# Hybrid diffusion step with mixture of experts: expert 2 loaded before the router has decided, the last two experts returned by one product, and products of constants in TensorE's waits

## The reference, cut to what matters

```python
h = _rms(x, p['norm2']) * (1 + sc2) + sh2
x = x + g2 * _hier_moe(h, p)
# _hier_moe: 4 groups x 4 experts; a token takes the best group, and in it the top 2 experts
gl = (h @ p['w_group_router']).astype(jnp.float32)
g_sel = jax.nn.one_hot(jnp.argmax(gl, axis=-1), N_GROUPS, dtype=jnp.float32)
top_v, top_i = lax.top_k(el_sel, TOP_K)
...
for gi in range(N_GROUPS):
    a = jnp.einsum('bsd,edf->bsef', h, p['w_e1'][gi])        # 1024 x 512 for each expert
    b = jnp.einsum('bsd,edf->bsef', h, p['w_e3'][gi])        # 1024 x 512
    y = y + jnp.einsum('bsef,efd->bsd', jax.nn.silu(a) * b * w_all[:, :, gi, :, None], p['w_e2'][gi])
```

## Time and profile before

| | us |
|---|---|
| median of 3 runs (1882.34 to 1887.23) | 1882.98 |
| the profiled execution, its own time | 1894.46 |
| its span in the profile | 1892.7 |
| PE busy in the span | 1782.1 (94%) |
| DVE, ACT, POOL busy | 813.7, 442.7, 122.4 |
| expert stage of layer 0, first hidden(0) product to last returned chunk | 704.5 to 976.0 |
| the same, layer 1 | 1607.8 to 1880.7 |

### The profile page before, as it was taken

The page is one execution under the profiler, slowest core; times in us unless marked ns, Lnnn a source line. Parts: engine busy times, 40 slices in busy tenths (PEclk is TensorE's granted clock), DMA queues, the critical chain, the costliest instruction groups (busy, mean ns, idle before and its releaser), DMA issues.

```text
span 1892.7 us, 25310 instructions
## 1 busy us (share of the span) xinstructions
PE 1782.1 (94%) x10202; PEld 1095.7 (58%) x10202; DVE 813.7 (43%) x1850; ACT 442.7 (23%) x956; POOL 122.4 (6%) x160
## 2 busy tenths in 40 slices
PE   6999999999999989997789999999999998999887
PEld 3445656688777773332245565667888877333223
DVE  1295473565544451111133966536655455111113
ACT  3312344333100121010043134334321112111002
POOL 0001201000000030000020020010000003000002
PEclk9999999999999989998989999999999998999988
DMA  9662293413556658999952221323123335899994
GB/s 403 224 261 91 95 361 106 156 68 112 198 221 270 245 200 353 425 427 426 424 209 101 110 94 58 131 93 120 69 90 112 133 151 201 326 424 425 428 427 156
DMA packets 51926, 422.42 MB, mean 223 GB/s; under 512 B 6448, under 2 KB 7872, under 8 KB 28768
## 3 DMA queue, kind: packets, MB, share of 16 engines
q1 hardware_dynamic: 33696, 369.35, 48.9%
q0 software_dynamic: 9632, 33.07, 5.1%
q10 hardware_dynamic: 8480, 18.35, 2.6%
HBM read 386.38 MB, written 32.28 MB: 221 GB/s over the span
## 4 chain that ended last, share of the span: by engine, by line
PE 81%; DMA 14%; another core or an unknown queue 1%; issue 1%; DVE 1%; ACT 1%; SPq 0%; POOL 0%; ACTq 0%; DVEq 0%
PE psum L871 19%; PE psum L1148 19%; PE psum L1137 9%; PE psum L1319 8%; PE psum L874 7%; DMA pc<-we_in 6%; DMA ring<-we_in 6%; PE psum L1340 2%; PE psum L791 2%; PE psum L1324 2%; DMA ring<-wch_in 2%; PE psum L849 1%; PE psum L1223 1%; PE psum L1335 1%
## 5 line engine op out<-in xcount | busy, mean ns | idle before, releaser
L871 PE MATMUL psum<-hT,ring 128*128 128x384 f32 x1088 | 363.9, 489 | 0.1
L871 PEld LDWEIGHTS psum<-hT,ring 128*128 128x128 f32 x1088 | 202.9, 190 | 141.2 <-issue 12.4
L1137 PE MATMUL psum<-pc,ring 128*128 128x384 f32 x512 | 175.6, 486 | 0.0
L1319 PE MATMUL psum<-ring,scr 128*64 128x512 f32 x512 | 126.9, 653 | 30.9 <-DMA ring<-we_in 27.1
L2625 DVE TENSOR_TENSOR ytok<-pc,psum 128x256 f32<-128x256 f32 (+1 forms) x32 | 15.1, 471 | 323.1 <-ACT pc L1815 323.1
L1148 PE MATMUL psum<-hT,ring 128*128 128x192 f32 x768 | 143.0, 329 | 1.8 <-ACT vals L1514 1.8
L1148 PEld LDWEIGHTS psum<-hT,ring 128*128 128x128 f32 x768 | 126.1, 190 | 18.6 <-issue 9.6
L1319 PE MATMUL psum<-pc,scr 128*64 128x512 f32 x512 | 118.0, 615 | 18.7 <-DMA pc<-we_in 18.7
L2015 DVE SCALAR_TENSOR_TENSOR pc<-pc,par 128x384 f32<-128x384 f32 x240 | 127.2, 605 | 0.0
L874 PE MATMUL psum<-ring,hT 128*128 128x512 f32 x288 | 125.2, 593 | 0.0
L1137 PEld LDWEIGHTS psum<-pc,ring 128*128 128x128 f32 x512 | 94.4, 190 | 51.9
(11 more groups left out here) (421 smaller groups left out, 2383.8 us busy)
## 6 DMA issues: line engine op xcount, KB each, us to landing
ring<-we_in SPq DMA_DIRECT2D x48, 2048.0 KB, 17.8
pc<-we_in SPq DMA_DIRECT2D x48, 2048.0 KB, 20.0
ring<-wch_in SPq DMA_DIRECT2D x18, 2048.0 KB, 8.3
ring<-wgate_in SPq DMA_DIRECT2D x16, 2048.0 KB, 8.4
ring<-wmod_in SPq DMA_DIRECT2D x18, 1024.0 KB, 6.7
pc<-wmod_in SPq DMA_DIRECT2D x24, 768.0 KB, 7.7
ring<-wbr_in SPq DMA_DIRECT2D x16, 1024.0 KB, 4.8
ring<-wtok_in SPq DMA_DIRECT2D x6, 2048.0 KB, 8.9
```

The lines of the kernel that those rows point to most:

```text
L871: mm = pe.matmul(F[:, 0:T], wv[:, k, n * P:(n + 1) * P], hT[:, k, :], start=k == 0, stop=k == KD - 1)
L1137: mm = pe.matmul(bank(7)[:, 0:T], wv[:, c, (n % 4) * P:(n % 4 + 1) * P], pc[:, MERGE_SLOT[i], c, :], start=c == 0, stop=c == 3)
L1319: mm = pe.matmul(bank(2)[BIG * h:BIG * h + BIG, :], x_h[:, k, 0:BIG], w[h][:, k, :], start=k == 0, stop=k == KD - 1, skip_group_check=True)
```

## The change

- **Expert 2 becomes fixed, expert 15 free** (`FREE = range(3, NE)`): expert 2 is wide whatever its load. Its two input blocks have places of their own, so that SP issues them before it waits for the sorted order.
- **Three deep instead of two.** Every third expert (2, 5, 8, 11, 14: `spare(e)`) has its input blocks in `spare_rooms`: parts of `par`, of the tile of `t_last` and `zeros`, a new tile `late_room` and `ytok`, four transfers in place of two. The others use slots 3 (e mod 3) + j. The input blocks of e + 3 are issued behind hidden(e). The output block keeps 3 (e mod 2) + 2.
- **The last two places, 14 and 15, hold the two least loaded experts** (`RANK_AT`), both narrow, and neither goes through the table. The results of 14 and 15 lie in the two halves of `x_pair`, and one product with both picks (`last_pickT`, now 128 rows instead of 96) adds them to a chunk. DVE has some 20 more small instructions in the router to build the picks. hidden(15) is issued before project(14), and `project(15)` has one part.
- **Gather.** POOL waits for the stores of experts 0 to 13 alone and gathers all three pairs without a further wait; `y_b` lies in `late_room`.
- **Constant products.** `constant_products(n)` puts n products of the identity with constants (128 x 512, into a bank that isn't read) ahead of waits: one before each of the six groups of transposes and one before the counts in the router; 3, 2 and 2 before the three waits for token sums at the stage's end.
- **Zeroing moves** from POOL's queue (behind the mLSTM states) to ACT's queue (at the start of the merge of layer 0), since the zeros' tile is now a weight room; SP waits for it before the early load of expert 2 in layer 0.
- The scratch room of POOL's descriptors shrinks to 4096 bytes a partition.

```diff
+def spare(e):
+    return e % 3 == 2
...
+def expert_slot(e, j):
+    return 3 * (e % 2) + 2 if j == 2 else 3 * (e % 3) + j
...
-FREE = range(2, NE - 1)
+FREE = range(3, NE)
...
-RANK_AT = (3, 4, 0, 5, 1, 6, 2, 7, 8, 9, 10, 11, 12)
+RANK_AT = (3, 0, 4, 1, 5, 2, 6, 7, 8, 9, 10, 11, 12)
...
+            def fill_spare(l, e):
+                for j, rooms in enumerate(spare_rooms):
+                    src, of = block_of(l, ("exp", e, j)), 0
+                    for room in rooms:
+                        width = room.shape[-1]
+                        sp.dma_start(room, src[:, of:of + width]).then_inc(rest_in.sem, 16)
+                        of += width
...
+                expert.clear()
+                if l == 0:
+                    sp.wait_ge(rows_zeroed.sem, 32)
+                fill_spare(l, 2)
+
                 sp.wait_ge(slot_ready.sem, slot_ready.at(l, 2))
-                expert.clear()
                 for e in range(NE - 1):
...
-                    if e < NE - 2:
+                    if e + 3 < NE:
                         sp.wait_ge(xab_done.sem, xab_done.at(l, e + 1))
-                        fill(l, ("exp", e + 2, 0))
-                        if e < NE - 3:
-                            fill(l, ("exp", e + 2, 1))
+                        fill_inputs(l, e + 3)
...
+            def constant_products(n):
+                for _ in range(n):
+                    pe.matmul(bank(6), ident, cst[:, 0:512], start=True, stop=True, skip_group_check=True)
...
                     for t in TURN_ORDER:
+                        constant_products(1)
...
+                constant_products(1)
                 pe.wait_ge(sel_ready.sem, sel_ready.at(l, 1))
...
+                hidden(NE - 1)
                 for n in range(2 if wide(NE - 2) else 1):
                     project(NE - 2, n)
-                hidden(NE - 1)
...
+                project(NE - 1, 0)
                 for t in range(2):
-                    project(NE - 1, t)
+                    constant_products(3 - t)
                     pe.wait_ge(mix_ready.sem, mix_ready.at(l, t + 1))
                     for n in range(KD - 2):
                         turn_back(n, t)
+                constant_products(2)
                 pe.wait_ge(mix_ready.sem, mix_ready.at(l, NT))
...
-                    pe.matmul(back_bank(n)[:, 0:T], x_last[:, n * P:(n + 1) * P], last_pickT[0:CAP, :], start=False, stop=True,
+                    pe.matmul(back_bank(n)[:, 0:T], x_pair[:, n * P:(n + 1) * P], last_pickT, start=False, stop=True,
...
+                if l == 0:
+                    ac.wait_ge(setup_s.sem, 7)
+                    for rows_d in (xs_d, ys_d):
+                        ac.dma_start(rows_d.rearrange("(p s) (a n) -> p (s a) n", p=P, n=256), ...)
...
-                for t in range(NT):
-                    scale_back(t)
-                for n in range(2):
-                    keep_last(n)
+                scale_back(0)
+                scale_back(1)
+                ac.wait_ge(xy_done.sem, xy_done.at(l, parts_to(NE)))
+                for c in range(2):
+                    ac.activation(x_pair[BIG:P, c * W:(c + 1) * W], bank(5)[BIG * c:BIG * c + BIG, :], ACT.Copy)
+                scale_back(2)
...
                 for t in range(NT):
-                    if t == 2:
-                        gp.wait_ge(xgt_done.sem, xgt_done.at(l, NE))
```

More of the change, by code:

```diff
@@ L117, in square_count @@
     return chunks + (1 + (before - 1) * KD if before else 0)
+def spare(e):
+    return e % 3 == 2
+SPARES = sum(spare(e) for e in range(NE))
+def expert_slot(e, j):
+    return 3 * (e % 2) + 2 if j == 2 else 3 * (e % 3) + j
 def weight_uses():
@@ L126, in weight_uses @@
         plan += [(("out", 0), 0), (("out", 1), 1)]
-        plan += [(("exp", e, j), 3 * (e % 2) + j) for e in range(NE) for j in range(3)]
+        plan += [(("exp", e, j), expert_slot(e, j)) for e in range(NE) for j in range(3) if j == 2 or not spare(e)]
         uses += [((l, key), slot) for key, slot in plan]
@@ L383, in hybrid_step @@
         y_a = [vals[:, t * D:(t + 1) * D] for t in range(NT)]
-        y_b = [ring[2][:, t * D:(t + 1) * D] for t in range(NT)]
+        y_b = [late_room[:, t * D:(t + 1) * D] for t in range(NT)]
         w_scaled = scr[:, 0:2 * KD * SUB].rearrange("p (c k n) -> p c k n", c=2, k=KD)
@@ L554, in hybrid_step @@
         xy_done = sig("expert_out_done", parts_to(NE))
-        xy_ready = sig("expert_out_ready", parts_to(NE))
-        y_stored = [sig(f"expert_out{i}_stored", (NE // 2 - i) * 16) for i in range(2)]
+        xy_ready = sig("expert_out_ready", parts_to(NE - 1) + 2)
+        y_stored = [sig(f"expert_out{i}_stored", (NE // 2 - 1) * 16) for i in range(2)]
         back_in = [sig(f"back_rows{t}_in", 32) for t in range(NT)]
@@ L621, in fill, with fill_inputs @@
                 sp.dma_start(ring[slot], block_of(l, key)).then_inc(slot_in[slot].sem, 16)
+            def fill_spare(l, e):
[5 more added lines that the diff above has]
+                        of += width
+            def fill_inputs(l, e):
+                if spare(e):
+                    fill_spare(l, e)
+                else:
+                    fill(l, ("exp", e, 0))
+                    fill(l, ("exp", e, 1))
             def fill_half(n):
@@ L1315, in hidden @@
                         pe.wait_ge(xg_ready.sem, xg_ready.at(l, e))
-                    w = [have(l, ("exp", e, j)) for j in range(2)]
+                    if spare(e):
+                        pe.wait_ge(rest_in.sem, 16 + 64 * (l * SPARES + e // 3 + 1))
+                        parts = [[r.rearrange("p (k n) -> p k n", n=512) for r in rooms] for rooms in spare_rooms]
+                        w = [[r[:, k, :] for r in rooms for k in range(r.shape[1])] for rooms in parts]
+                    else:
+                        w = [[have(l, ("exp", e, j))[:, k, :] for k in range(KD)] for j in range(2)]
                     for k in range(KD):
                         for h in range(2):
-                            mm = pe.matmul(bank(2)[BIG * h:BIG * h + BIG, :], x_h[:, k, 0:BIG], w[h][:, k, :],
+                            mm = pe.matmul(bank(2)[BIG * h:BIG * h + BIG, :], x_h[:, k, 0:BIG], w[h][k],
                                            start=k == 0, stop=k == KD - 1, skip_group_check=True)
@@ L1873, in _ @@
               .then_inc(setup_s.sem, 1)
-            ve.memset(zeros[:, :], 0.0)
+            ve.memset(zeros, 0.0)
             ve.memset(room32[:, :], float(CAP - BIG))
+            ve.memset(last_ones[:, :, :], 0.0)
             ve.memset(small[:, 60:62], 0.0).then_inc(setup_s.sem, 1)
@@ L2582, in _ @@
                 chain.settle()
-                step(ve.memset(rmul[:, :, NE - 1:NE], 1.0))
+                for i in range(2):
+                    step(ve.tensor_scalar(last_ones[:, i, FREE.start:FREE.stop], rank, float(RANK_AT[i - 2]), None, ALU.is_equal))
                 chain.settle()
+                of_last = [last_ones[:, i:i + 1, :].to_broadcast([P, NT, NE]) for i in range(2)]
+                for i in range(2):
+                    step(ve.tensor_tensor(rmul[:, :, :], rmul[:, :, :], of_last[i], ALU.max))
+                    chain.settle()
                 for k, w in enumerate((w1, w2)):
```

84 lines of the change are left out of this document (44 added, 40 removed).

## The result

| | median, us | runs | ratio to before |
|---|---|---|---|
| before | 1883.39 | 1882.34 to 1887.23, 4 runs | |
| changed kernel | **1901.26** | 1898.82 to 1902.29, 4 runs | 1.0089, interval 1.0072 to 1.0107 |

The changed kernel is slower, by 17.9 us, where 20 us less were forecast. Its profiled execution took 1901.25 us, with a span of 1899.5, just its median.

What follows compares the result with a forecast made beforehand. Expert weights by DMA (some 425 GB/s), not PE, were taken to bound the expert stages. Terms of -9.9, +2.5 and -2.6 gave -10.0 us a layer, -20 in all: 1863.0 us from a median of 1882.98, range 1852 to 1876.

Steps and rivals of the forecast that it cites:

- Zeroing: Start of layer 0's merge: transfers stay hidden, their issue costs ACT 0 to 2.6 us once, taken as 0.
- ACT is held by its queue: Rival, start of the merge: ACT stands until 6144-piece transfers drain, some 28 us of PE's time, 1891 us; chance 0.04.
- The sum: Whole kernel: 2 x -10.0 = -20 us, profiled 1894.5 to 1874.5; against the median of 1882.98, 1863.0.
- Terms 1 to 3: Expert stage: two blocks leave the stream, -9.9; new hole, +2.5; behind the last weights, -2.6; together -10.0 us a layer.
- Term 2: Behind wide hidden(2): the weight stream runs dry near 744.5, a new hole of +2.5 us, bounds 0 and 5.
- Constant products: Router and stage end: gain and cost between -4.5 and +2.6 us for hidden(0)'s start, taken as 0.
- clock held: Rival, router and stage end: products keep the clock up, hidden(0) 2 to 4 us earlier, 1851 us; chance 0.17.
- DVE's additions: Router: some 20 instructions, 4 to 5 us, covered by PE's one-hot products and hidden(0): cost nothing.
- early load beside the scatter: Router: expert 2's early blocks overlap the scatter by some 2 us, slack 2.3: cost 0, bounds 0 and 7.6.
- Slow tail: Rival, stage end: PE's waits lower the clock, chunks run at half clock, +4 to +6 a layer, 1873 us; chance 0.12.
- traffic: Rival, router: the early load only moves traffic; scatter, rows and stream 7.6 us late, 1878 us; chance 0.04.
- late load: Rival: zeroes or the merge's end hold the early load behind the router; only the tail gains, 1872 us; chance 0.03.

Runs made afterwards that it cites:

- before_2: The kernel before, unchanged, run again for a second profile: 1883.48 us, ratio 1.0008; its profiled execution took 1881.26 us.
- z_big_3: The kernel of z_big, unchanged, run a third time on another chip: 1872.44 us against 1883.73 for the kernel before, ratio 0.995.
- z_apart: Changed kernel with the second table's zeroing transfer issued much later in the merge's loop: 1871.07 us against 1882.37 for before, ratio 0.9942.
- z_big: Changed kernel, zeroing a table in 512 pieces of 12 KB, not 6144 of 1 KB: 1876.37 us against 1891.27 for before, ratio 0.9926.
- z_big_2: The kernel of z_big run again as base for its variants: 1876.41 us against 1892.15 for the kernel before, ratio 0.9928.
- load_late: z_big with the inputs of expert 2 loaded behind hidden(0), not behind expert 1's output block: 1888.90 us, ratio 0.9984 to before.
- z_before_act: Kernel before with only the two zeroing transfers moved from POOL to ACT ahead of the merge: 1916.40 us against 1891.27, ratio 1.012.

## Why the prediction was wrong

**Two of its steps failed. The stage then ended when it was forecast to, in part by luck.** Of the miss of 38.3 us (1901.3 against 1863.0) the hold is 24.3 and the base 11.5.

*Zeroing failed.* It said "I take 0", with 0 to 2.6 us as its bounds, from the 0.5 us of ACT's other transfers and POOL's 2.2. Measured: 24.3 us by the traces, 25.1 by the runs, twice. The bound was drawn from the wrong rows. All other transfers of ACT are of 128 to 384 KB, one sixteenth or less of these 6144 KB, and the two on POOL's queue are issued by another engine. The prediction did see the mechanism, as the rival "ACT is held by its queue" with 28 us, and its test ("a gap over 3 us") was met by the first rows read. It gave the rival 0.04 since "issues take 0.5 us whatever the size so far". The size meant there was bytes, and no row had this number of pieces behind another such transfer. The unknown cost was one-sided and large, and the bounds should have reached to 28. The rival's mechanism was right up to what drains: most of the first transfer, not both. The Trainium skill (DMA: Bandwidth & Descriptors, Issuing engine by pattern) says that the hardware queues of SP and ACT are generally faster than POOL's; for this pair the trace disagrees: the first issue took 2.24 us on POOL, the second 26.28 on ACT, and the second table landed 49.4 us behind its issue from POOL and 48.8 from ACT.

*The sum failed.* It took 20 us off the profiled execution (1894.5) and then the same 20 off the median, 11.5 us lower. But most of the 11.5 lay in the two stretches that the change works on (5.6 and 5.4, before_2), and an ordinary execution of before has them no more. Against it the forecast end of the chunks, 966.0, is 5 us earlier and not 10: before_2's last chunk product starts at 970.50. From router to next layer z_big_3 (683.55 to 972.22, 1575.58 to the span's end at 1870.2) gains 3.7 and 4.9 us on before_2, half of the 10.0 forecast. The gain without the hold is 11.3 us on two chips (z_apart, z_big_3) and 14 to 16 on the chip where before takes 1891 to 1892. 1894.5 - 20 = 1874.5 was the better forecast of such a kernel: z_big_3 has 1872.4, z_big 1876.4.

*Terms 1 to 3 held as a timeline.* Without the hold the return of layer 0 falls on the forecast. PE, POOL and ACT in z_big_3:

```profile
929.20 5.35 PE L1382 MATMUL psum<-pc,mva 128*64 128x512 f32 x16 [3.64 <-DMA pc<-we_in]
934.85 7.09 PE L1365 MATMUL psum<-ring,scr 128*64 128x512 f32 x32
965.86 0.81 PE L1469 MATMUL psum<-gaT,scr 128*128 128x384 f32 x2
```
```profile
944.66 1.05 POOL L2849 DMA_INDIRECT vals<-expert_out_rows,slot_back  x1 [236.65 <-DMA expert_out_rows<-scr]
951.24 1.00 POOL L2849 DMA_INDIRECT late_room<-expert_out_rows,slot_back  x1 [0.30 <-issue]
```
```profile
936.15 0.48 ACTq L1851 DMA_DIRECT2D expert_out_rows<-scr  x1
957.44 1.15 ACT L1893 ACTIVATE vals<-vals,rt 128x1024 f32<-128x1024 f32 x1 [0.15 <-DMA late_room<-expert_out_rows,slot_back]
```

| | forecast | z_big_3 |
|---|---|---|
| project(13) | 929.5 | 929.20 |
| store of 13 issued | 934.8 | 936.15 |
| first, sixth gather | 945.1, 951.7 | 944.66, 951.24 |
| last scaling | 957.1 | 957.44 |
| chunks end | 966.0 | 966.5 |

Term 2's hole shows as a lower rate (353 GB/s in 748 to 755 of z_big_2), and the net of terms 1 and 2 is 7.4 us a layer, against 6.2 measured by load_late. But the end of the weights, from which term 3 reckons, was missed. It was to be 939.2, with project(13) two blocks ahead of it. SP issued the last block only here:

```profile
934.73 0.33 SPq L638 DMA_DIRECT2D pc<-we_in  x1
```

That is behind project(13), whose place it takes; it landed 8.8 us later, at 943.5, and from 932 to 934 the rate was 82 GB/s. The return hangs on project(13) and not on that block, so the end stood; that 929.5 was met from a wrong end of the stream is luck. The idle time of PE for weights fell from 51.5 to 34.5 us, by a third and not by half. And the lower bound of the range of a layer, -16, leaves out term 2 at 0: its own bounds give -18.

*Constant products* at nothing: right within the measurement where before runs at 1883 (3.3 us, not told apart), but by luck. The router in z_big_3:

```profile
693.78 1.02 PE L808 MATMUL psum<-cst 128*128 128x512 f32 x2
694.64 0.32 PE L1335 MATMUL psum<-sel,cst 128*128 128x48 f32 x2
696.71 5.57 PE L1401 MATMUL psum<-mod_rows,vals 128*128 128x96 f32 x48 [0.44 <-DVE mod_rows L2575]
```

The trace has two records for one float32 product of 512 columns (x2), so one costs 0.86 us (693.78 to 694.64) and not the 0.43 that the prediction read from 288 records. The counts (L1335) came 11.1 us behind the router's first product, 7.6 in before: 3.5 us later, outside the bound of 2.6. The one-hot products started 2.5 us later than 694.23, which was a named sign of being wrong, and the scatter 2.5 us later (700.43). At the full clock the one-hot products then took 5.57 us and not 8.82, which gave it back. Where before runs at 1891 the absence of the products cost more, towards "clock held", which had a chance of 0.17.

*DVE's additions* and the *early load beside the scatter*: nothing of them showed as a loss of its own, but little could. hidden(0) began 19.6 us behind the router's first product in z_big_3 and 22.9 in z_big_2, 20.7 in before and 18.6 in before_2: a loss of one or two us can hide in that spread. The first load of 128 KB of rows behind the scatter landed in 2.8 us with the early load (z_big_2) and 2.6 without it (load_late). DVE's additions had no run of their own. *Slow tail*, *traffic* and *late load* did not come true.

## What to carry to other kernels

What a transfer costs the engine that issues it went here by the pieces already in that queue; it could not be read from smaller transfers. Moving the bulk transfers onto an engine that others wait for cost nothing with few large pieces, or with transfers spaced out. The rest of this change gained 11 us, less than the one row of 26 us took.

A profiled execution that lies well off the median has its excess somewhere: find out whether it is in the stretch that the change touches, before a gain read from it is taken off the median.

Count how many records the trace makes of one instruction of the program before a cost is read from their mean.

## What the runs showed that was not expected

- Two transfers of 6144 pieces of 1 KB issued by ACT one behind the other: the first takes 0.72 us to issue, the second 26.2; with 3072 in the first 18.0; with 3072 in the second 26.2. With 512 pieces of 12 KB each: 0.73 and 0.65 us, and landings at the same time.
- ACT goes on when 956 to 1051 pieces of the first transfer are left, in four kernels with a hold.
- The kernel before has medians 9 us apart between chips (1882.4 and 1891.3), the kernel without the hold only 4 us (1872.4 and 1876.4). Where before takes 1882.4, its project(15) ran at the full clock (3.65 us); where it takes 1891.3, z_before_act, which shares that code, shows 6.13 and 5.90 us for it. But both profiles that show project(15) at the half clock are of executions 10 us or more above the median of their kernel, and one of them is before's first, where the median was 1883. Whether the half clock goes with the chip is not shown.
